# Matrix memory of a two-block model on one core: first head's scores ahead of the gate rows, each head's row spread behind its scores, gate exponential ahead of two value evictions

## The chip, the cores and the metric

One core of a Trainium2 chip runs the whole kernel in one launch. The metric is the device time of an execution in microseconds (us), and the smaller the better. All arithmetic is in 32-bit floats.

## The reference, cut to what matters

The model is a chain of several mixers and feed-forward networks over 256 tokens of width 1024. The change lies in the first mixer alone, a matrix memory (mLSTM) of 4 heads of width 512:

```
xm, z = split(u @ w_in)
xc = silu(causal_conv(xm));  q, k = block_diag(xc);  v = block_diag(xm)
i_pre, f_pre = split(q @ wg_q + k @ wg_k + v @ wg_v + b_gates)
b = cumsum(log_sigmoid(f_pre));  d_log = causal(b[t] - b[s] + i[s])
m_t = max(..., max_s d_log)
scores = (q k^T) * exp(d_log - m_t)
h = (scores v) / max(|sum_s scores|, exp(-m_t))
out = ((layer_norm(h) * norm_w + skip * xc) * silu(z)) @ w_out
```

For each head and each token t, the row values m_t and exp(-m_t) must reach all 128 partitions, since the kernel keeps the keys s on the partitions and the tokens t along the free axis.

## The kernel before, in words

The program is written engine by engine: TensorE (PE), VectorE (DVE), ScalarE (ACT), GpSimd (POOL) and SyncE (SP) each have one list of instructions, executed in the order in which it is written, and semaphores tie them together. There is no planner; the order of the text is the order of the work.

**Banks.** Most PE products go to four PSUM banks in turn. Every product (or group) is a numbered "job" from the list JOBS (line 216); job j uses bank j modulo 4. `wait_free(pe, j)` makes PE wait until job j-4 has been read out, `full` tells that job j is complete, `wait_full(engine, j)` lets the reader wait for that, `out_of` tells that it has been read, and `wait_out` waits for the reading.

**Weights.** SP loads tiles of 1 MB into a ring of six slots (`ring`, line 807), each load released when PE has begun the tile that lets the slot go. Between the pieces of the matrix memory PE executes steps of another product, `ada_step("b", ...)` (matmul at line 1062): the modulation vectors that later layers need. They use two tiles each and a bank of their own, so they wait for nothing of the matrix memory.

**The order on PE around the change** (`stage_mlstm`, from line 1209): query products (1269) with the gate sums (1275), one ada step, the selection of gate rows (1286), eight groups of value products `m_v` (1294), one ada step, the transposed column values `m_cT` (1303), then `m_rows`: for each of the 4 heads one matmul (1309) that spreads two rows of the gates, of 256 tokens each, over the 128 partitions, with 4 rows of contraction and 512 columns. Only then comes the loop over heads: scores (1325, 8 matmuls), one ada step, the sum of the scores (1333), the scores times the values in two groups (1342), the variance of the head before (`head_var`, 1316), one ada step. Every 32-bit matmul stands in the trace as two records, so the 4 row spreads are 8 records.

**DVE** (from 2923) makes the gate rows (2925 to 2947), copies the column values (2950) and the four spread rows out of PSUM (2955), scales the value sums (2984), and adds the causal mask to the first head's row (`decays(0)`, 2962) and centres its values (`centre_values(0)`, 2969). In the head loop it multiplies scores and decay (2992), forms the divisor (2995 to 3000), divides the two groups of outputs (3004), and does `decays(h+1)`, `centre_values(h+1)` and then, from h = 1 on, `head_scale(h-1)` (2974 to 2981: reciprocal and two products over 1024 columns). PE's sum of the scores (1333) waits for 2992.

**ACT** evicts the queries (2293), computes exp and log for the gates (2296, 2299), evicts the eight value groups (2303), then takes the exponential of one gate row (2305), on which 1303 waits, and in the head loop the exponential of the decay (2309), the squares (2339) and the root (2344).

Of the kernel before, what the change touches and what calls it, by code (L numbers as in the profile page):

```python
# [7 lines left out]
P = 128  # L8
F32 = mybir.dt.float32
ALU = mybir.AluOpType  # L10
ACT = mybir.ActivationFunctionType
# [4 lines left out]
T = 256  # L16
# [6 lines left out]
IC = DI // P  # L23
NH = 4
DH = DI // NH
HC = DH // P
# [181 lines left out]
UNDER_INPUT, FIRST_INPUT = 10, 6  # L208
TILES = [("ada_a", 8), ("m_in0", FIRST_INPUT)]
for _s in range(UNDER_INPUT):  # L210
# [3 lines left out]
         ("ada_gap1", 4), ("ffn2", 34), ("ada_gap2", 4), ("hg_z", 8), ("hg_q", 4), ("hg_i", 4), ("hg_g", 4), ("hg_o", 4),  # L214
         ("ffn3", 34)]
JOBS = [("params", 1), ("xT", 4), ("late_params", 4), ("m_in", 2 * INPUT_TILES), ("m_qk", 16), ("m_fsel", 1),
        ("m_v", 8), ("m_cT", 1), ("m_rows", NH), ("m_head", 4 * NH),
        ("m_out", 4), ("ln0", 4), ("ffn0", 4 * FSTEPS - 2), ("s_bT", 8), ("s_cT", 4), ("ln1", 4),
        ("s_direct", 1), ("s_pair", NPAIR), ("glu", 8), ("ln2", 4), ("router", 1), ("u_tok", 4), ("places", 1), ("ctxT", 4), ("ln3", 4), ("rms0", 3),
        ("mla_seq", len(MLA_SEQ) - AH // 2), ("mla_o", 8), ("rms1", 3),  # L220
# [4 lines left out]
def build_program(nc, w, const, out):  # L225

    _, cols = shape_constants()
    tile_of, job_of = reserve(TILES), reserve(JOBS)

    with ExitStack() as ctx:  # L230
        signals = {}

        def S(name):

            if name not in signals:
                signals[name] = ctx.enter_context(nc.semaphore(name))
            return signals[name]
# [93 lines left out]
        def in_job(j):  # L331

            return job_of["m_in"] + 2 * j

        def ffn_job(n):

# [108 lines left out]
        def key_block(a, s):  # L445

            return a[:, s * T:s * T + (P if s else T)]
# [563 lines left out]
        def _(pe):  # L1011
# [197 lines left out]
            def stage_mlstm():  # L1209
# [79 lines left out]
                for g in range(8):  # L1289
# [4 lines left out]
                        last = pe.matmul(bank(j)[:, c * P:(c + 1) * P], xm[:, c0 + c, 4 + a * P:4 + (a + 1) * P],  # L1294
                                         bd[:, 2, c0 + c], start=True, stop=True)
                    full(last, j)
                ada_step("b", UNDER_INPUT + 1, 1)

                j = job_of["m_cT"]
                wait_free(pe, j)  # L1300
                pe.wait_ge(S("gate_rows_ready"), 1)
                for a in range(2):
                    last = pe.matmul(bank(j)[:, a * NH:(a + 1) * NH], gate_rows[0:NH, 4, a * P:(a + 1) * P],
                                     ident[0:NH, 0:NH], start=True, stop=True)
                full(last, j)
                for h in range(NH):
                    j = job_of["m_rows"] + h
                    wait_free(pe, j)
                    full(pe.matmul(bank(j), ident[0:NH, h:h + 1].broadcast_to([NH, P]),
                                   gate_rows[0:NH, 5:7].rearrange("p a t -> p (a t)"), start=True, stop=True), j)  # L1310

                def head_var(h):

# [2 lines left out]
                        last = pe.matmul(psum[:, VAR, 0:T], ones, hsq[:, k], start=k == 0, stop=k == HC - 1)  # L1316
                    last.then_inc(S("h_var_full"), 1)

                wait_out(pe, job_of["m_qk"] + IC - 1)
                for h in range(NH):  # L1320
                    j = job_of["m_head"] + 4 * h
                    wait_free(pe, j)
                    for s in range(2):
                        for c in range(HC):
                            last = pe.matmul(key_block(bank(j), s), xc[:, h * HC + c, s * P:(s + 1) * P],
                                             qk[:, h * HC + c, 0, s * P:T], start=c == 0, stop=c == HC - 1)
                    full(last, j)
                    ada_step("b", UNDER_INPUT + 2 + 2 * h, 1)

                    wait_out(pe, j)  # L1330
                    wait_free(pe, j + 1)
                    for s in range(2):
                        last = pe.matmul(bank(j + 1)[:, s * P:T], ones, key_block(scor[:, h % 2], s), start=s == 0, stop=s == 1,
                                         skip_group_check=True)
                    full(last, j + 1)
                    pe.wait_ge(S("v_centred"), h + 1)
                    for g in range(2):
                        wait_free(pe, j + 2 + g)
                        for e in range(2):
                            for s in range(2):  # L1340
                                at = h * DH + (2 * g + e) * P
                                last = pe.matmul(bank(j + 2 + g)[:, e * T + s * P:(e + 1) * T], vbuf[:, s, at:at + P],
                                                 key_block(scor[:, h % 2], s), start=s == 0, stop=s == 1,
                                                 skip_group_check=True)
                        full(last, j + 2 + g)
                    if h:
                        head_var(h - 1)
                    ada_step("b", UNDER_INPUT + 3 + 2 * h, 1)
# [882 lines left out]
        def _(act):  # L2231
# [36 lines left out]
            def stage_mlstm():  # L2268
# [30 lines left out]
                act.activation(gate_rows[0:NH, 2], gate_rows[0:NH, 2], ACT.Ln, bias=one[0:NH, 0:1]).then_inc(S("ln_f_ready"), 1)  # L2299
                for g in range(8):  # L2300
                    j, s, h = job_of["m_v"] + g, g // 4, g % 4
                    wait_full(act, j)
                    out_of(act.activation(vbuf[:, s, h * DH:(h + 1) * DH], bank(j), ACT.Copy, accum_out=v_sums[:, s, h:h + 1]), j)
                act.wait_ge(S("m_sum_ready"), 1)
                act.activation(gate_rows[0:NH, 6], gate_rows[0:NH, 6], ACT.Exp, scale=-1.0).then_inc(S("gate_rows_ready"), 1)
                for h in range(NH):
                    for s in range(2):
                        act.wait_ge(S("decay_sum_ready"), 2 * h + s + 1)
# [26 lines left out]

            def head_squares(h):

                wait_out(act, job_of["m_head"] + 4 * h + 3)
                act.activation(hsq, hT[:, h * HC:(h + 1) * HC], ACT.Square).then_inc(S("h_sq_ready"), 1)

            def head_root(h):
# [380 lines left out]
        def _(dve):  # L2722
# [136 lines left out]
            def stage_mlstm():  # L2859
# [85 lines left out]
                dve.drain()  # L2945
                dve.tensor_tensor(g[0:NH, 6], g[0:NH, 3], g[0:NH, 5], ALU.add)
                dve.tensor_scalar(g[0:NH, 5], g[0:NH, 5], -1.0, None, ALU.mult).then_inc(S("m_sum_ready"), 1)
                j = job_of["m_cT"]
                wait_full(dve, j)
                out_of(dve.tensor_copy(cT, bank(j)[:, 0:2 * NH].rearrange("p (s h) -> p s h", s=2)), j)  # L2950
                wait_out(dve, job_of["m_qk"] + IC - 1)
                for h in range(NH):
                    j = job_of["m_rows"] + h
                    wait_full(dve, j)
                    out_of(dve.tensor_copy(nm[:, h], bank(j).rearrange("p (k t) -> p k t", k=2)), j)
                dve.wait_ge(S("tables_in"), 16)
                causal = c_("causal").rearrange("p (s t) -> p s t", s=2)

                def decays(h):

                    for s in range(2):
                        dve.tensor_tensor(key_block(decay, s), nm[:, h, 0, s * P:T], causal[:, s, s * P:T], ALU.add
                                          ).then_inc(S("decay_sum_ready"), 1)
# [8 lines left out]
                def head_scale(h):  # L2972
# [7 lines left out]
                    dve.drain()  # L2980
                    dve.tensor_tensor(hh, hh, zs[:, h * HC:(h + 1) * HC], ALU.mult).then_inc(S("h_scaled"), 1)

                wait_out(dve, job_of["m_v"] + 7)
                dve.tensor_scalar(v_sums, v_sums, -1.0 / DH, None, ALU.mult)
                dve.drain()
                decays(0)
                centre_values(0)
                for h in range(NH):
                    j = job_of["m_head"] + 4 * h
                    dve.wait_ge(S("decay_ready"), 2 * h + 2)  # L2990
                    wait_full(dve, j)
                    out_of(dve.scalar_tensor_tensor(scor[:, h % 2], bank(j)[:, 0:CAUSAL], DH ** -0.5, decay, ALU.mult, ALU.mult), j)
                    wait_full(dve, j + 1)

                    dve.tensor_tensor(recip_[:, 0], bank(j + 1)[:, 0:T], nm[:, h, 1], ALU.max)
                    dve.drain()
                    out_of(dve.scalar_tensor_tensor(recip_[:, 0], bank(j + 1)[:, 0:T], -1.0, recip_[:, 0],
                                                    ALU.mult, ALU.max), j + 1)
                    dve.drain()
                    dve.reciprocal(recip_[:, 1], recip_[:, 0])  # L3000
                    dve.drain()
                    for g in range(2):
                        wait_full(dve, j + 2 + g)
                        out_of(dve.tensor_tensor(hT[:, h * HC + 2 * g:h * HC + 2 * g + 2],
                                               bank(j + 2 + g).rearrange("p (a t) -> p a t", a=2),
                                               recip_[:, 1:2].broadcast_to([P, 2, T]), ALU.mult), j + 2 + g)
# [1021 lines left out]
```

## Time and profile before

| | |
|---|---|
| three runs | 2701.3, 2708.13 and 2711.41 us, median 2708.13 |
| span of the profiled execution | 2713.5 us, 5.4 above that median |
| PE busy | 2625.8 us of the span |
| DVE, ACT, POOL busy | 909.8, 404.2, 910.4 us |
| matrix memory from the last query products to the output product | about 184 to 252 us of the span |
| mean granted clock of TensorE | 0.989 of full |

The time of the profiled execution outside its span is not listed. In the profile a line gives the start of a merged group of records, its length, the engine, the line of the code, what it writes and reads, and how often; idle time ahead of it stands in square brackets with what released it. The ends of matmuls are modelled, so lengths are best read as differences between starts.

### The profile page before, as it was taken

What the parts mean: (1) busy time and instruction counts of PE and PEld (TensorE: products, weight loads), DVE (VectorE), ACT (ScalarE), POOL (GpSimd) and SP (SyncE); (2) the same over time, 40 slices, a digit from 0 to 9 for tenths busy, and PEclk for the clock granted to TensorE, in tenths of its full rate; (3) what the DMA queues carried; (4) which work ended last, traced back from release to release, by engine and by line L of the source; (5) the groups of instructions that cost most, each with busy time, mean ns of one, the idle gap of its engine ahead of it and who ended that gap; (6) DMA issues with size and microseconds to landing.
All of it is one profiled execution on the core that took longest, in us unless ns stands there. A gap on an engine that the chain in (4) does not pass through costs nothing.

```text
span 2713.5 us, 47220 instructions
## 1 busy us (share of the span) xinstructions
PE 2625.8 (97%) x20645; PEld 1863.1 (69%) x20645; DVE 909.8 (34%) x1647; ACT 404.2 (15%) x839; POOL 910.4 (34%) x715
## 2 busy tenths in 40 slices
PE   8999999989999999999999999999999999999998
PEld 6767799956644444334445446488888778998998
DVE  4746422384300011100013583222221136522651
ACT  0132010120311000100002344100000121221000
POOL 2662168584000000000000350145555331612886
PEclk9999999999999999999999999999999999999999
DMA  9978545478499999999997210323222243122552
GB/s 299 320 250 287 135 162 164 149 264 280 156 376 407 407 381 385 391 399 406 385 384 249 79 38 16 124 78 93 80 83 86 89 129 109 58 67 93 171 163 87
DMA packets 318303, 561.88 MB, mean 207 GB/s; under 512 B 45544, under 2 KB 181520, under 8 KB 317968
## 3 DMA queue, kind: packets, MB, share of 16 engines
q1 hardware_dynamic: 299280, 554.57, 57.4%
q10 hardware_dynamic: 18816, 4.27, 0.8%
q8 instruction: 164, 2.69, 0.4%
q14 instruction: 43, 0.35, 0.0%
HBM read 557.75 MB, written 1.05 MB: 206 GB/s over the span
## 4 chain that ended last, share of the span: by engine, by line
PE 50%; issue 36%; POOLq 4%; POOL 4%; DVE 2%; DVEq 1%; ACT 1%; DMA 1%; SPq 0%; ACTq 0%
PE psum L1937 10%; PE psum L2166 5%; PE psum L1974 5%; PE psum L2020 4%; PE psum L1021 3%; PE psum L1406 3%; PE psum L2194 2%; PE psum L1359 2%; PE psum L2040 2%; PE psum L1753 2%; POOLq L3767 2%; PE psum L1419 1%; PE psum L2067 1%; PE psum L1244 1%; PE psum L1062 1%
## 5 line engine op out<-in xcount | busy, mean ns | idle before, releaser
L1614 PE MATMUL psum<-ring,xe 128*32 128x512 f32 (+1 forms) x4608 | 458.0, 557 | 2.0 <-issue 1.4
L1614 PEld LDWEIGHTS psum<-ring,xe 128*32 128x32 f32 x4608 | 156.4, 110 | 291.1 <-issue 255.4
L3906 POOL TENSOR_TENSOR ckv<-ckv,nstat 128x512 f32<-128x512 f32 x2 | 2.5, 1265 | 889.9 <-DVE nstat L3413 889.9
L3304 DVE TENSOR_TENSOR act_in<-act_in,psum 128x256 f32<-128x256 f32 (+1 forms) x72 | 28.7, 399 | 629.5 <-ACT act_in L2474 629.5
L1636 PE MATMUL psum<-ring,zs 128*32 128x256 f32 x4224 | 232.3, 379 | 0.2 <-DMA ring<-in_moe_w 0.2
L1636 PEld LDWEIGHTS psum<-ring,zs 128*32 128x32 f32 x4224 | 141.7, 110 | 92.7 <-issue 5.5
L3919 POOL TENSOR_TENSOR w_sums<-ring 128x512 f32<-128x512 f32 (+1 forms) x34 | 42.4, 1247 | 298.1 <-DVE ctxT L3470 124.1
L2474 ACT ACTIVATE act_in<-psum 128x256 f32<-128x256 f32 (+1 forms) x72 | 26.4, 367 | 567.9 <-PE psum L1614 567.9
L1753 PE MATMUL psum<-a,ring 128*128 128x512 f32 x224 | 97.5, 594 | 2.0 <-ACT a L2523 1.3
L3413 DVE RECIPROCAL nstat<-nstat 128x512 f32<-128x512 f32 x23 | 75.8, 3328 | 43.0 <-ACT nstat L2235 43.0
L1937 PE MATMUL psum<-a,w_sums 128*128 128x256 f32 x352 | 83.2, 379 | 2.0 <-ACT a L2523 2.0
L1021 PE MATMUL psum<-a,ring 128*128 128x256 f32 x384 | 84.4, 380 | 0.4 <-DVE a L3669 0.3
L1937 PE MATMUL psum<-a,ring 128*128 128x256 f32 x352 | 80.7, 380 | 2.2 <-DVE a L3384 2.2
L1753 PEld LDWEIGHTS psum<-a,ring 128*128 128x128 f32 x224 | 42.1, 190 | 56.0 <-issue 51.8
L3998 POOL TENSOR_TENSOR w_sums<-ring 128x512 f32<-128x512 f32 (+1 forms) x34 | 42.3, 1244 | 112.1 <-PE psum L2166 51.7
L1021 PEld LDWEIGHTS psum<-a,ring 128*128 128x128 f32 x384 | 72.4, 190 | 10.8 <-DVE a L3669 1.2
L1937 PE MATMUL psum<-x_rows,w_sums 128*128 128x256 f32 x352 | 79.6, 379 | 0.0
L1419 PE MATMUL psum<-zs,ring 128*128 128x256 f32 x352 | 77.8, 379 | 0.0
L1937 PEld LDWEIGHTS psum<-a,ring 128*128 128x128 f32 x352 | 66.5, 190 | 12.3 <-DVE a L3384 2.8
L1937 PEld LDWEIGHTS psum<-a,w_sums 128*128 128x128 f32 x352 | 66.8, 190 | 11.4 <-issue 2.4
L1937 PEld LDWEIGHTS psum<-x_rows,w_sums 128*128 128x128 f32 x352 | 66.9, 190 | 9.1
L1419 PEld LDWEIGHTS psum<-zs,ring 128*128 128x128 f32 x352 | 66.0, 190 | 8.5
(612 smaller groups left out, 4892.6 us busy)
## 6 DMA issues: line engine op xcount, KB each, us to landing
ring<-in_moe_w SPq DMA_DIRECT2D x216, 1024.0 KB, 11.2
ring<-in_ffn_w SPq DMA_DIRECT2D x97, 1024.0 KB, 5.2
ring<-in_ada_w SPq DMA_DIRECT2D x96, 1024.0 KB, 8.4
ring<-in_moe_w SPq DMA_DIRECT2D x64, 768.0 KB, 6.6
ring<-in_hg_w_in SPq DMA_DIRECT2D x20, 1024.0 KB, 5.1
ring<-in_mlstm_w_in SPq DMA_DIRECT2D x16, 1024.0 KB, 9.2
ring<-in_mlstm_w_out SPq DMA_DIRECT2D x8, 1024.0 KB, 7.7
ring<-in_s_w_glu SPq DMA_DIRECT2D x8, 1024.0 KB, 11.7
```

Of the source, the lines that this page charges most:

```text
L1021: last = pe.matmul(bank(j)[:, n * T:(n + 1) * T], tile[:, k * width + n * P:k * width + (n + 1) * P], src(k), start=start and k == 0, stop ...
L1359: last = pe.matmul(bank(j)[:, n * T:(n + 1) * T], ring[:, t % RING, k * 256 + n * P:k * 256 + (n + 1) * P], hT[:, 8 * half + k], start=hal ...
L1406: last = pe.matmul(ffn_product(n, m), held[:, k], moving(k), start=k == 0, stop=k == 3)
L1419: last = pe.matmul(psum[:, NB + n // 2, (n % 2) * T:(n % 2 + 1) * T], ring[:, t % RING, k * D + n * P:k * D + (n + 1) * P], hid[:, i % 2, ...
L1614: last = pe.matmul(psum[rows, r, 0:2 * nb * 32].rearrange("p (u b f) -> p u b f", u=2, b=nb), xe[:, k, at:at + 32], tile[:, :, :, rows], s ...
L1636: last = pe.matmul(psum[32 * b:32 * b + 32, DOWN + r // 2, (r % 2) * T:(r % 2 + 1) * T], turned[:, r, at:at + 32], ring[:, t % RING, a:a + T],
L1753: last = pe.matmul(bank(j), ring[:, t % RING, at:at + P], src(k), start=k == 0, stop=k == kc - 1)
L1937: last = pe.matmul(product_bank(side, m), held[:, k], moving(k), start=k == 0, stop=k == 3)
L1974: last = pe.matmul(product_bank(q, m), held[:, k, q], moving(2 * kk + k), start=kk == 0 and k == 0 and m in (1, 5, 3, 6), stop=kk == 5, sk ...
L2020: last = pe.matmul(product_bank(side, m), held[:, k], moving(k), start=k == 0, stop=k == 3)
L2166: last = pe.matmul(small_bank(side, m), held[:, k], moving(k), start=k == 0, stop=k == 3)
L3413: dve.reciprocal(st, st).then_inc(S("nrstd_ready"), 1)
```

## The change

It renumbers the jobs: `m_cT`, `m_rows` and the 16 head jobs, 21 in all, become one list of 21 in the new order of use. On PE the first head's scores come directly behind the value products; then the column values; then the row spread of head 0; then the ada step that stood in front of the column values. In the head loop, each further head's row spread stands directly behind its scores. On DVE, the copy of a head's spread rows moves into `decays(h)`, with a drain behind it; `decays(0)` moves ahead of the wait for the last value eviction. The places of the calls `decays(h+1)`, `centre_values(h+1)` and `head_scale(h-1)` in the DVE loop stay. On ACT, the gate exponential moves from behind the eighth value eviction to between the sixth and the seventh. Every matmul, copy and activation of before is still there; the only new instructions are the four drains on DVE, one behind each copy.

```
-        ("m_v", 8), ("m_cT", 1), ("m_rows", NH), ("m_head", 4 * NH),
+        ("m_v", 8), ("m_head", 5 * NH + 1),

+        def head_job(kind, h):
+            return job_of["m_head"] + {"scores": 5 * h + 1 if h else 0, "cT": 1, "rows": 5 * h + 2, "sums": 5 * h + 3,
+                                       "values": 5 * h + 4}[kind]

 PE, behind the value products:
-                ada_step("b", UNDER_INPUT + 1, 1)
-                j = job_of["m_cT"]
+                def head_scores(h):
+                    j = head_job("scores", h)
+                    wait_free(pe, j)
+                    for s in range(2):
+                        for c in range(HC):
+                            last = pe.matmul(key_block(bank(j), s), xc[:, h * HC + c, s * P:(s + 1) * P],
+                                             qk[:, h * HC + c, 0, s * P:T], start=c == 0, stop=c == HC - 1)
+                    full(last, j)
+                def head_rows(h):
+                    j = head_job("rows", h)
+                    wait_free(pe, j)
+                    full(pe.matmul(bank(j), ident[0:NH, h:h + 1].broadcast_to([NH, P]),
+                                   gate_rows[0:NH, 5:7].rearrange("p a t -> p (a t)"), start=True, stop=True), j)
+                wait_out(pe, job_of["m_qk"] + IC - 1)
+                head_scores(0)
+                j = head_job("cT", 0)
                 wait_free(pe, j)
                 pe.wait_ge(S("gate_rows_ready"), 1)
...
-                for h in range(NH):
-                    j = job_of["m_rows"] + h
-                    wait_free(pe, j)
-                    full(pe.matmul(bank(j), ident[0:NH, h:h + 1].broadcast_to([NH, P]), ...), j)
+                head_rows(0)
+                ada_step("b", UNDER_INPUT + 1, 1)
...
                 for h in range(NH):
...
-                    ada_step("b", UNDER_INPUT + 2 + 2 * h, 1)
-                    wait_out(pe, j)
+                    if h:
+                        head_scores(h)
+                        head_rows(h)
+                    ada_step("b", UNDER_INPUT + 2 + 2 * h, 1)
+                    j = head_job("sums", h)
+                    wait_out(pe, head_job("scores", h))

 ACT:
                 for g in range(8):
                     j, s, h = job_of["m_v"] + g, g // 4, g % 4
+                    if g == 6:
+                        act.wait_ge(S("m_sum_ready"), 1)
+                        act.activation(gate_rows[0:NH, 6], gate_rows[0:NH, 6], ACT.Exp, scale=-1.0).then_inc(S("gate_rows_ready"), 1)
                     wait_full(act, j)
                     out_of(act.activation(vbuf[:, s, h * DH:(h + 1) * DH], bank(j), ACT.Copy, accum_out=v_sums[:, s, h:h + 1]), j)
-                act.wait_ge(S("m_sum_ready"), 1)
-                act.activation(gate_rows[0:NH, 6], ..., ACT.Exp, scale=-1.0).then_inc(S("gate_rows_ready"), 1)

 DVE:
-                for h in range(NH):
-                    j = job_of["m_rows"] + h
+                dve.wait_ge(S("tables_in"), 16)
+                causal = c_("causal").rearrange("p (s t) -> p s t", s=2)
+                def decays(h):
+                    j = head_job("rows", h)
                     wait_full(dve, j)
                     out_of(dve.tensor_copy(nm[:, h], bank(j).rearrange("p (k t) -> p k t", k=2)), j)
-                dve.wait_ge(S("tables_in"), 16)
-                causal = c_("causal").rearrange("p (s t) -> p s t", s=2)
-                def decays(h):
+                    dve.drain()
                     for s in range(2):
                         dve.tensor_tensor(key_block(decay, s), nm[:, h, 0, s * P:T], causal[:, s, s * P:T], ALU.add
...
+                decays(0)
                 wait_out(dve, job_of["m_v"] + 7)
                 dve.tensor_scalar(v_sums, v_sums, -1.0 / DH, None, ALU.mult)
                 dve.drain()
-                decays(0)
                 centre_values(0)
```

## Rows read from the trace of the kernel before

**Rows 1.** The page: busy us of each engine, share of the span, instructions.

```profile
PE 2625.8 (97%) x20645; PEld 1863.1 (69%) x20645; DVE 909.8 (34%) x1647; ACT 404.2 (15%) x839; POOL 910.4 (34%) x715
```

**Rows 2.** PE in order of time, 195 to 232 us: start, length, group, count.

```profile
195.24 1.92 PE L1062 MATMUL psum<-ring,csil_one 128*32 128x512 f32 x16
197.90 0.57 PE L1303 MATMUL psum<-cst,act_in 4*128 4x4 f32 x4 [0.74 <-ACT act_in L2305]
198.34 4.83 PE L1309 MATMUL psum<-act_in,cst 4*128 4x512 f32 x8
203.10 5.06 PE L1325 MATMUL psum<-qk,xc 128*128 128x256 f32 x16
...
209.94 0.92 PE L1333 MATMUL psum<-bd,cst 128*128 128x256 f32 x4
...
215.26 2.88 PE L1325 MATMUL psum<-qk,xc 128*128 128x256 f32 x16
218.08 1.92 PE L1062 MATMUL psum<-ring,csil_one 128*32 128x512 f32 x16
219.94 0.92 PE L1333 MATMUL psum<-bd,cst 128*128 128x256 f32 x4
...
225.13 1.92 PE L1062 MATMUL psum<-ring,csil_one 128*32 128x512 f32 x16
...
229.80 1.92 PE L1062 MATMUL psum<-ring,csil_one 128*32 128x512 f32 x16
231.66 0.92 PE L1333 MATMUL psum<-bd,cst 128*128 128x256 f32 x4
```

**Rows 3.** PE's weight loads in order of time, during the row spreads.

```profile
199.29 0.18 PEld L1309 LDWEIGHTS psum<-act_in,cst 4*128 4x128 f32 x1 [0.24 <-issue]
199.72 0.18 PEld L1309 LDWEIGHTS psum<-act_in,cst 4*128 4x128 f32 x1 [0.24 <-issue]
```

**Rows 4.** Stretches: from:to, us, busy of PE, PEld, DVE, ACT, POOL; granted clock, DMA share, GB/s.

```profile
159.10:163.60 4.50, 4.50 (x25) 4.50 (x26) 1.57 (x8) 1.59 (x4) 0.01 (x1) 0.62 0.89 329
195.30:197.20 1.90, 1.86 (x17) 0.35 (x16) 0.00 (x0) 1.84 (x3) 1.90 (x3) 1.00 0.00 0
201.00:203.10 2.10, 2.10 (x4) 0.34 (x2) 0.72 (x2) 0.00 (x0) 2.10 (x3) 0.50 1.05 396
203.10:208.10 5.00, 5.00 (x19) 4.16 (x19) 2.46 (x6) 0.80 (x2) 5.00 (x6) 0.55 0.05 18
```

**Rows 5.** ACT in order of time, 194 to 198 us.

```profile
194.45 0.60 ACT L2303 ACTIVATE vbuf<-psum 128x512 f32<-128x512 f32 x1 [0.18 <-PE psum L1294]
...
196.05 1.28 ACT L2305 ACT_TABLE_LOAD   x1
197.34 0.41 ACT L2305 ACTIVATE act_in<-act_in 4x256 f32<-4x256 f32 x1
```

**Rows 6.** DVE in order of time, 194 to 231 us.

```profile
194.09 0.39 DVE L2947 TENSOR_SCALAR act_in<-act_in 4x256 f32<-4x256 f32 x1
...
203.21 0.69 DVE L2955 COPY bd<-psum 128x512 f32<-128x512 f32 x1 [1.01 <-PE psum L1309]
...
204.59 1.15 DVE L2969 TENSOR_SCALAR vbuf<-vbuf,small 128x512 f32<-128x512 f32 x2
...
224.94 0.62 DVE L2962 TENSOR_TENSOR bd<-bd,cst 128x256 f32<-128x256 f32 x2
...
226.26 1.75 DVE L2976 RECIPROCAL bd<-bd 128x256 f32<-128x256 f32 x1
228.08 1.23 DVE L2978 TENSOR_TENSOR qk<-qk,bd 128x1024 f32<-128x1024 f32 x1
...
230.53 0.55 DVE L2992 SCALAR_TENSOR_TENSOR bd<-psum,bd 128x384 f32<-128x384 f32 x1
```

**Rows 7.** PE in order of time, 159 to 172 us: input products behind a wait for POOL.

```profile
159.08 4.57 PE L1244 MATMUL psum<-qk 128*128 128x128 f32 x24 [2.66 <-POOL qk L3780]
...
169.11 2.84 PE L1244 MATMUL psum<-qk 128*128 128x128 f32 x24
```

More of the change, by code:

```diff
@@ L1305, in stage_mlstm @@
                 full(last, j)
-                for h in range(NH):
-                    j = job_of["m_rows"] + h
-                    wait_free(pe, j)
-                    full(pe.matmul(bank(j), ident[0:NH, h:h + 1].broadcast_to([NH, P]),
-                                   gate_rows[0:NH, 5:7].rearrange("p a t -> p (a t)"), start=True, stop=True), j)
+                head_rows(0)
+                ada_step("b", UNDER_INPUT + 1, 1)
                 def head_var(h):
@@ L1317, in head_var @@
                     last.then_inc(S("h_var_full"), 1)
-                wait_out(pe, job_of["m_qk"] + IC - 1)
                 for h in range(NH):
-                    j = job_of["m_head"] + 4 * h
+                    if h:
[4 more added lines that the diff above has]
+                    wait_out(pe, head_job("scores", h))
                     wait_free(pe, j)
                     for s in range(2):
-                        for c in range(HC):
-                            last = pe.matmul(key_block(bank(j), s), xc[:, h * HC + c, s * P:(s + 1) * P],
-                                             qk[:, h * HC + c, 0, s * P:T], start=c == 0, stop=c == HC - 1)
+                        last = pe.matmul(bank(j)[:, s * P:T], ones, key_block(scor[:, h % 2], s), start=s == 0, stop=s == 1,
+                                         skip_group_check=True)
                     full(last, j)
-                    ada_step("b", UNDER_INPUT + 2 + 2 * h, 1)
-                    wait_out(pe, j)
[L1331 to L1335, printed above, removed]
                     pe.wait_ge(S("v_centred"), h + 1)
+                    j = head_job("values", h)
                     for g in range(2):
-                        wait_free(pe, j + 2 + g)
+                        wait_free(pe, j + g)
                         for e in range(2):
@@ L1341, in stage_mlstm @@
                                 at = h * DH + (2 * g + e) * P
-                                last = pe.matmul(bank(j + 2 + g)[:, e * T + s * P:(e + 1) * T], vbuf[:, s, at:at + P],
+                                last = pe.matmul(bank(j + g)[:, e * T + s * P:(e + 1) * T], vbuf[:, s, at:at + P],
                                                  key_block(scor[:, h % 2], s), start=s == 0, stop=s == 1,
                                                  skip_group_check=True)
-                        full(last, j + 2 + g)
+                        full(last, j + g)
                     if h:
@@ L2301, in stage_mlstm @@
                     j, s, h = job_of["m_v"] + g, g // 4, g % 4
+                    if g == 6:
+                        act.wait_ge(S("m_sum_ready"), 1)
+                        act.activation(gate_rows[0:NH, 6], gate_rows[0:NH, 6], ACT.Exp, scale=-1.0).then_inc(S("gate_rows_ready"), 1)
                     wait_full(act, j)
                     out_of(act.activation(vbuf[:, s, h * DH:(h + 1) * DH], bank(j), ACT.Copy, accum_out=v_sums[:, s, h:h + 1]), j)
-                act.wait_ge(S("m_sum_ready"), 1)
-                act.activation(gate_rows[0:NH, 6], gate_rows[0:NH, 6], ACT.Exp, scale=-1.0).then_inc(S("gate_rows_ready"), 1)
                 for h in range(NH):
@@ L2336, in head_squares @@
             def head_squares(h):
-                wait_out(act, job_of["m_head"] + 4 * h + 3)
+                wait_out(act, head_job("values", h) + 1)
                 act.activation(hsq, hT[:, h * HC:(h + 1) * HC], ACT.Square).then_inc(S("h_sq_ready"), 1)
@@ L2947, in stage_mlstm @@
                 dve.tensor_scalar(g[0:NH, 5], g[0:NH, 5], -1.0, None, ALU.mult).then_inc(S("m_sum_ready"), 1)
-                j = job_of["m_cT"]
+                j = head_job("cT", 0)
                 wait_full(dve, j)
@@ L2951, in stage_mlstm @@
                 wait_out(dve, job_of["m_qk"] + IC - 1)
-                for h in range(NH):
-                    j = job_of["m_rows"] + h
-                    wait_full(dve, j)
-                    out_of(dve.tensor_copy(nm[:, h], bank(j).rearrange("p (k t) -> p k t", k=2)), j)
                 dve.wait_ge(S("tables_in"), 16)
@@ L2959, in decays @@
                 def decays(h):
+                    j = head_job("rows", h)
+                    wait_full(dve, j)
+                    out_of(dve.tensor_copy(nm[:, h], bank(j).rearrange("p (k t) -> p k t", k=2)), j)
+                    dve.drain()
                     for s in range(2):
@@ L2985, in stage_mlstm @@
                 dve.drain()
-                decays(0)
                 centre_values(0)
                 for h in range(NH):
-                    j = job_of["m_head"] + 4 * h
+                    j = head_job("scores", h)
                     dve.wait_ge(S("decay_ready"), 2 * h + 2)
@@ L2992, in stage_mlstm @@
                     out_of(dve.scalar_tensor_tensor(scor[:, h % 2], bank(j)[:, 0:CAUSAL], DH ** -0.5, decay, ALU.mult, ALU.mult), j)
-                    wait_full(dve, j + 1)
-                    dve.tensor_tensor(recip_[:, 0], bank(j + 1)[:, 0:T], nm[:, h, 1], ALU.max)
+                    j = head_job("sums", h)
+                    wait_full(dve, j)
+                    dve.tensor_tensor(recip_[:, 0], bank(j)[:, 0:T], nm[:, h, 1], ALU.max)
                     dve.drain()
-                    out_of(dve.scalar_tensor_tensor(recip_[:, 0], bank(j + 1)[:, 0:T], -1.0, recip_[:, 0],
-                                                    ALU.mult, ALU.max), j + 1)
+                    out_of(dve.scalar_tensor_tensor(recip_[:, 0], bank(j)[:, 0:T], -1.0, recip_[:, 0],
+                                                    ALU.mult, ALU.max), j)
                     dve.drain()
@@ L3001, in stage_mlstm @@
                     dve.drain()
+                    j = head_job("values", h)
                     for g in range(2):
-                        wait_full(dve, j + 2 + g)
+                        wait_full(dve, j + g)
                         out_of(dve.tensor_tensor(hT[:, h * HC + 2 * g:h * HC + 2 * g + 2],
-                                               bank(j + 2 + g).rearrange("p (a t) -> p a t", a=2),
-                                               recip_[:, 1:2].broadcast_to([P, 2, T]), ALU.mult), j + 2 + g)
+                                               bank(j + g).rearrange("p (a t) -> p a t", a=2),
+                                               recip_[:, 1:2].broadcast_to([P, 2, T]), ALU.mult), j + g)
                     if h + 1 < NH:
```

## The prediction

> **What bounds the kernel now.** I read the page first. PE is busy for 2625.8 of 2713.5 us [rows 1], so what counts is what keeps PE waiting or slow. Then PE's list in order of time around the change [rows 2], PE's weight loads there [rows 3], the granted clock by stretches [rows 4], and ACT's and DVE's lists [rows 5, 6], each to see which of them is late where PE waits. The span lies 5.4 us above the median of the runs; all sums below are differences against the profiled execution, put on the median of 2708.13. A measurement of this kernel can tell about 0.5% from no change, 13.5 us.
>
> Three things are to be seen. First, ahead of the heads PE waits 0.74 us for the gate exponential, since ACT loads its table (1.28 us) and computes it (0.41 us) only behind the last value eviction, though DVE had delivered its input at 194.09 + 0.39 [rows 2, 5, 6]. Second, the column values and the four spreads use 4 of 128 rows, and behind them the clock falls: 0.50 (1.2 of 2.4 GHz) from 201.0 to 203.1, 0.55 until 208.1 [rows 4]. The scores of head 0 start at 203.10 and their successor sums only at 209.94; the scores of head 1 take 218.08 - 215.26 = 2.82 us, those of head 0 take 5.06 by their length [rows 2]. Third, in the loop PE runs gapless: from the sums of head 1 (219.94) to those of head 2 (231.66) are 11.72 us [rows 2], and DVE finishes what the sums wait for at 230.53 + 0.55 = 231.08 [rows 6]. **DVE is only 0.6 us ahead of PE there**, and it is free to be so because its next mask addition starts at 224.94 [rows 6] on a row that was spread long before.
>
> **Part 1, the first head.** Before, PE needs 209.94 - 195.24 = 14.70 us from the ada step to the sums. At full clock the same work is: ada step with the wait, 197.90 - 195.24 = 2.66; column values 198.34 - 197.90 = 0.44; four spreads; scores 2.82; one ada step, 231.66 - 229.80 = 1.86 [rows 2]. A record of a spread takes 199.72 - 199.29 = 0.43 us, a spread of two records 0.86, four 3.44 [rows 3]. Sum 11.22, so the slow clock cost 3.48.
> After, from 195.24: scores 2.82, column values 0.44, one spread 0.86, two ada steps 3.72, sum 7.84, and the sums start at 203.08, **6.86 us earlier**. Of it 2.58 are three spreads that come back later, about 0.8 the wait, 3.5 the clock.
> The covers: ACT's table load starts when its sixth eviction is out, about 194.3 (the row at 194.45 is the seventh); 1.28 + 0.41 give 196.0 [rows 5], and PE wants it at 195.24 + 2.82 = 198.06. Two value evictions move behind it and end near 197.3; their reader, DVE's scaling of value sums, comes after 200. That edit costs nothing while 2 us of scores cover it; uncovered it would cost at most its 1.69. DVE gets the spread at 199.36; before, from the start of its last copy to the start of centring are 204.59 - 203.21 = 1.38 us, then centring 1.15 and the product 0.55 (the loop's) [rows 6]; with 0.1 for signals the sums could start at 202.6. PE's 203.08 is later, by 0.5.
> The ada steps' weights: DMA stands still at 195.3 to 197.2 [rows 4], so the ring is full when they are wanted later than before. I cost the move of the ada step past SP's queue at nothing. Were the ring short by a tile, a megabyte at the 396 GB/s of rows 4 is 2.6 us; the longer loop below makes that less likely.
>
> **Part 2, head 1.** The spread adds 0.86 to PE. DVE stands in `decays(1)` until it is complete, then needs: signal 0.05, copy 0.69, drain 0.07 (228.08 - 226.26 - 1.75), then what is 230.53 + 0.55 - 224.94 = 6.14 in the loop, less the head scaling that head 1 has not (230.53 - 226.26 = 4.27), so 1.87, and 0.1 back to PE: 2.78 [rows 6]. PE covers one ada step, 1.86. Wait 0.92. **Later by 1.8.**
>
> **Part 3, heads 2 and 3.** The added wait is `wait_full` on the spread inside `decays(h+1)`. Queued behind it on DVE stand the copy, the mask, `centre_values`, the whole `head_scale` of the head before, and the product that the next sums wait for. None of these but the first two needs the spread. PE delivers the spread only behind variance, ada step and scores: for head 2 at (229.80 - 219.94) + 0.86 = 10.72 us after the sums of head 1 [rows 2], while DVE used to go on at 224.94, 5.0 after them. From there 0.05 + 0.69 + 0.07 + 6.14 + 0.1 = 7.05 us, of which PE covers 1.86: it waits 5.2 us. With the spread, 6.05 for each head, twice: **later by 12.1.** ACT's exponential lies beside centring and scaling, as before. POOL's additions and the output product follow DVE as before; nothing behind head 3 takes it back, since the loads follow PE's progress and the ring is full.
>
> **Part 4, the clock of the two waits.** What falls behind a wait of 5.2 us is not in the loop of before. From below, nothing: the 0.74 us wait ahead of 197.90 was itself followed by full clock [rows 2, 4]. From above, by a row: behind a wait of 2.66 us for POOL the same 24 records took 4.57 instead of 2.84, 1.73 us more, at a granted 0.62 [rows 4, 7]; behind the dip at 201 the scores took 5.06 instead of 2.88, 2.2 more [rows 2]. Both rows are nearer to a 5.2 us wait than the short one, so I take their middle, 1.95, twice: 3.9. The Trainium skill speaks against this change here (TensorE: Matmul & The Clock Gate, section on HAM oscillation): a loop whose matmul bursts are parted by long waits falls to 1.2 GHz and pays the ramp again in every turn. By it both waits pay in full; the trace agrees so far as its 2.66 us wait did.
>
> **Sum.** -6.86 + 1.8 + 12.1 + 3.9 = +10.9. Predicted 2708.1 + 10.9 = 2719, which is 0.4% slower, within what counts as the same. Without a clock price it is +7.0 (2715), with 2.2 twice +11.4.
>
> **The rivals.**
> *The slow clock lasts through the burst.* Behind each wait the sums, values and variance are 225.13 - 219.94 = 5.2 us at full clock [rows 2]. If all of it runs at 1.2 GHz, each wait costs 5.2 more instead of 1.95: +7.0 + 10.4 = +17.4, 2725.5. This ends on the slower side. Its place is the stretch from the sums of heads 2 and 3 to the next ada step, and it decides once the dips cost over 3.2 us each. For it: the first dip lasted from about 201 to 208 [rows 4]. Against: dense work ended it, and each stall here is followed by dense work.
> *The wait of DVE is covered.* If the copy came early enough, only part 1 and three spreads would remain, -6.86 + 2.58 = -4.3, 2704. Against it: PE's text puts the spread behind the scores and DVE's text puts everything behind the spread, and no engine reorders its list in these rows.
> *The first head gains no clock.* Column values, a spread and two ada steps follow the first scores; if the clock falls there as before, 3.5 come back: +14.4, 2722.5. For it: 1.3 us of 4-row work. Against: that was 3.9 us before, behind a wait, and scores now stand ahead of it.
>
> **How the numbers follow.** The forecast 0.67, the lasting slow clock 0.18, no gain of clock at the first head 0.08, the covered wait 0.07. The forecast's own range is its clock from 0 to 2.2 with the runs' own spread of some 5 us: 2710 to 2725. The range takes in the rival above: 2709 to 2727. Slower by over 0.5%: all of the lasting clock, half of the third rival, and 0.05 of the forecast by its edge, 0.27. Faster by over 0.5% is left only if something unseen is added to the covered wait, 0.03. The same: 0.70.
>
> **What would show it.** In the new profile: the sums of head 0 start near 203; a full granted clock from 199 to 207; DVE's copy of each spread row waits for PE, the second to fourth for 4 to 6 us; PE waits about 0.9 us at the sums of head 1 and about 5 at those of heads 2 and 3, released by DVE's product of scores and decay; the sums stand some 17.8 us apart for heads 1 to 2 and 2 to 3 in place of 11.72; a dip of granted clock behind each of these two. It would be wrong if the head loop were still gapless, if the sums of head 0 came at 206 or later, or if DMA released any of these waits.

## The result, and the profile after

The changed kernel takes 2717.5 us (median of 6 runs, 2714.81 to 2724.47) against 2706.2 us of the kernel before (6 runs, 2701.3 to 2711.41): ratio 1.0047, interval 1.0034 to 1.006. That is slower by 11.3 us by the medians and by some 13 by the ratio. The forecast was 2719, 10.9 above the median that the first three runs of before had (2708.13), in the range 2709 to 2727.

Both profiled executions reach this part at slightly different times (the changed one 4.98 us earlier). Of that, 1.6 us are the dip of the clock in the input products [rows 7], which its execution didn't have; the rest comes from elsewhere ahead of this part and is not followed up. So everything below is told from landmarks inside the part: from the end of the value products, where PE turns to the ada step (before) or to the first scores (after), to the start of the output product. That was 252.16 - 195.24 = 56.92 us before, and is 260.60 - 190.26 = 70.34 now, **13.4 longer**.

PE in order of time in the changed kernel; columns are start, length, group, count, and in brackets the idle time ahead with what released it (L1309 scores, L1326 column values, L1317 spread, L1067 ada step, L1349 sums, L1359 values, L1336 variance, L1376 output product):

```profile
190.26 2.78 PE L1309 MATMUL psum<-qk,xc 128*128 128x256 f32 x16
192.97 0.60 PE L1326 MATMUL psum<-cst,act_in 4*128 4x4 f32 x4
193.44 1.10 PE L1317 MATMUL psum<-act_in,cst 4*128 4x512 f32 x2
194.47 3.64 PE L1067 MATMUL psum<-ring,csil_one 128*32 128x512 f32 x32
198.21 0.92 PE L1349 MATMUL psum<-bd,cst 128*128 128x256 f32 x4
...
210.58 0.92 PE L1349 MATMUL psum<-bd,cst 128*128 128x256 f32 x4 [1.26 <-DVE bd L3011]
...
220.45 1.12 PE L1317 MATMUL psum<-act_in,cst 4*128 4x512 f32 x2
221.50 1.92 PE L1067 MATMUL psum<-ring,csil_one 128*32 128x512 f32 x16
228.60 1.65 PE L1349 MATMUL psum<-bd,cst 128*128 128x256 f32 x4 [5.17 <-DVE bd L3011]
230.04 4.75 PE L1359 MATMUL psum<-bd,vbuf 128*128 128x256 f32 x16
234.62 1.89 PE L1336 MATMUL psum<-bd,cst 128*128 128x256 f32 x8
...
249.26 1.65 PE L1349 MATMUL psum<-bd,cst 128*128 128x256 f32 x4 [5.17 <-DVE bd L3011]
...
260.60 14.06 PE L1376 MATMUL psum<-qk,ring 128*128 128x256 f32 x64
```

Against [rows 2]: the first four lines are gapless and at full clock, where the kernel before waited and then ran slow. But the loop, gapless before, now has a wait of 1.26 us and two of 5.17 us, all for L3011, DVE's product of scores and decay. And behind the long waits PE is slow: the 16 values take 4.75 in place of 2.78.

Stretches of the same profile (from:to, us, busy of PE, PEld, DVE, ACT, POOL, then granted clock, DMA share, GB/s): the first head, the first long wait with what follows it, and what follows the second.

```profile
190.26:198.21 7.95, 7.85 (x56) 4.07 (x54) 3.47 (x8) 2.78 (x8) 7.63 (x8) 1.00 0.17 41
...
223.40:228.60 5.20, 0.03 (x5) 0.00 (x1) 4.99 (x6) 2.49 (x3) 0.44 (x1) 0.87 1.04 384
228.60:236.45 7.85, 7.85 (x29) 6.59 (x29) 3.98 (x5) 0.00 (x0) 1.91 (x1) 0.65 0.18 64
249.26:257.02 7.76, 7.76 (x28) 6.50 (x29) 3.98 (x5) 0.00 (x0) 1.90 (x1) 0.66 0.23 74
```

PE is idle while DVE is busy all through the wait; the clock falls within it (0.87 as the mean of the wait), and sums, values and variance take 7.85 and 7.76 us at a granted 0.65 and 0.66, where the same work took 5.19 before (219.94 to 225.13 in [rows 2]).

What DVE does around the first long wait, in order of time (L2977 copy of the spread, L2981 mask, L2988 centring, L2995 to L3000 head scaling, L3011 product):

```profile
221.61 0.69 DVE L2977 COPY bd<-psum 128x512 f32<-128x512 f32 x1 [5.94 <-PE psum L1317]
222.40 0.63 DVE L2981 TENSOR_TENSOR bd<-bd,cst 128x256 f32<-128x256 f32 x2
222.94 0.88 DVE L2988 TENSOR_SCALAR vbuf<-vbuf,small 128x512 f32<-128x512 f32 x2
223.73 1.75 DVE L2995 RECIPROCAL bd<-bd 128x256 f32<-128x256 f32 x1
225.55 1.23 DVE L2997 TENSOR_TENSOR qk<-qk,bd 128x1024 f32<-128x1024 f32 x1
226.85 1.23 DVE L3000 TENSOR_TENSOR qk<-qk,zs 128x1024 f32<-128x1024 f32 x1
227.99 0.55 DVE L3011 SCALAR_TENSOR_TENSOR bd<-psum,bd 128x384 f32<-128x384 f32 x1
```

The two engines wait for each other by turns: DVE stands 5.94 us for a spread that PE places behind its scores, then PE stands 5.17 us for work that DVE had queued behind that spread. In [rows 6] DVE went from the values of a head into the mask without a wait.

### The profile page after: what moved, and what is told of

Its sections match the earlier page's. It is cut to its first block, busy times and chain, and to the rows that moved or that the text cites. A ratio compares the mean times of both kernels' runs of the same rounds, so it can differ in the third digit from the quotient of the medians.

```text
span 2719.6 us, 47223 instructions
## 1 busy us (share of the span) xinstructions
PE 2622.0 (96%) x20645; PEld 1859.2 (68%) x20645; DVE 905.6 (33%) x1647; ACT 403.7 (15%) x839; POOL 911.3 (34%) x715
## 3 DMA queue, kind: packets, MB, share of 16 engines
HBM read 557.75 MB, written 1.05 MB: 205 GB/s over the span
## 4 chain that ended last, share of the span: by engine, by line
PE 48%; issue 36%; POOLq 5%; POOL 4%; DVE 4%; DVEq 1%; ACT 1%; DMA 1%; SPq 0%; ACTq 0%
PE psum L1954 10%; PE psum L2183 5%; PE psum L1991 5%; PE psum L2037 3%; PE psum L1026 3%; PE psum L1423 3%; PE psum L2211 2%; PE psum L1376 2%; PE psum L2057 2%; PE psum L1770 2%; POOLq L3788 2%; PE psum L1436 1%; PE psum L2084 1%; POOLq L3928 1%; PE psum L1890 1%
```

## The experiments

Each is told by its ratio to the kernel before and by the same local time, from the end of the value products to the output product.

**1. Head scaling ahead of the wait for the spread.** DVE's order alone is changed:

```
-                    if h + 1 < NH:
-                        decays(h + 1)
-                        centre_values(h + 1)
                     if h:
                         head_scale(h - 1)
+                    if h + 1 < NH:
+                        decays(h + 1)
+                        centre_values(h + 1)
```

> The changed kernel with one thing altered on DVE: in the head loop head_scale(h-1) stands ahead of decays(h+1) and centre_values(h+1). Theory (DVE's in-order wait for the spread holds up work that doesn't need it): head scaling is then done while the spread is still to come, and only copy, mask, centring and product stay behind it. PE's waits at the sums of heads 2 and 3 fall from 5.17 us to about 1.3, as at head 1; sums of head 1 to sums of head 2 take about 14.2 us in place of 18.02; the clock doesn't fall there. From the sums of head 0 to the output product some 13 us shorter than in the changed kernel; the whole about 0.5 us over the kernel before, ratio to it 1.000. Rival (the reading of the spread itself, or the extra drain, is what is slow): the waits stay over 4 us and the ratio stays 1.0047.

Measured: ratio 1.0011 (1.0002 to 1.002); local time 243.84 - 185.90 = 57.94 us, 12.4 less than the changed kernel and 1.0 more than before. PE around head 2:

```profile
206.22 0.92 PE L1349 MATMUL psum<-bd,cst 128*128 128x256 f32 x4 [1.26 <-DVE bd L3011]
...
220.65 0.92 PE L1349 MATMUL psum<-bd,cst 128*128 128x256 f32 x4 [1.59 <-DVE bd L3011]
221.41 2.78 PE L1359 MATMUL psum<-bd,vbuf 128*128 128x256 f32 x16
```

From sums to sums are 14.43 us in place of 18.02, and the values behind a wait of 1.59 take their full-clock 2.78. The spread is as late as ever; only the 4.3 us of scaling no longer stand behind it. From the sums of head 0 to the output product the changed kernel takes 20.2 us more than before (62.39 against 42.22), and this order of work on DVE takes 12.4 of them away, as the theory had it. What is left of them is the three spreads, 3.2 us, and three short waits, 4.4. The ratio is 0.001 over the one named. The wait is 0.3 longer than expected: POOL now runs at the same time as the mask, which takes 0.7 us more by it, while the centring, slowed at head 1, is not slowed here (see the last section).

**2. The spread ahead of variance, ada step and scores.** DVE stays as changed, the job numbers of spread and scores change places, and on PE:

```
                         full(last, j + g)
+                    if h + 1 < NH:
+                        head_rows(h + 1)
                     if h:
                         head_var(h - 1)
...
                     if h:
                         head_scores(h)
-                        head_rows(h)
```

> The changed kernel with the spread of head h+1 put right behind the values of head h, ahead of variance, ada step and scores; the job numbers follow. Theory (the spread comes too late, not too dear): DVE finds it ready when it gets there, no wait of PE in the head loop, 11.72 + 1.05 = 12.8 us from the sums of head 1 to those of head 2, no fall of the clock. Against the kernel before: -6.75 us at the first head and three spreads of 1.05 us back, -3.6 us, ratio 0.9987; against the changed kernel -17 us. Rival (splitting the spreads over the loop costs by itself, by small matmuls between large ones or by the clock): no faster than the kernel before, ratio 1.001 or more.

> The kernel with the spread behind the values once more, since its interval touched 1.0. If its local gain of 3.2 us is real in the whole time, the ratio is again 0.998 to 0.9995; if that was chance, it is 1.000 or more.

Measured: 0.9991 (0.9982 to 1.0) the first time, 0.9988 (0.9979 to 0.9997) the second. Local times 238.96 - 185.25 = 53.71 and 243.31 - 189.59 = 53.72 us, 3.2 less than before, where 3.6 were expected. PE, first run:

```profile
204.25 0.92 PE L1348 MATMUL psum<-bd,cst 128*128 128x256 f32 x4
205.01 2.78 PE L1358 MATMUL psum<-bd,vbuf 128*128 128x256 f32 x16
207.72 1.12 PE L1317 MATMUL psum<-act_in,cst 4*128 4x512 f32 x2
...
217.22 0.92 PE L1348 MATMUL psum<-bd,cst 128*128 128x256 f32 x4
```

and DVE in the same time, which copies the spread (L2978) without a wait:

```profile
208.05 1.29 DVE L3026 TENSOR_TENSOR qk<-psum,bd 128x512 f32<-128x512 f32 x2
209.26 0.68 DVE L2978 COPY bd<-psum 128x512 f32<-128x512 f32 x1
```

No wait is left: 217.22 - 204.25 = 12.97 from sums to sums. The change's gain at the first head is real and is kept here; its loss was the place of three small matmuls. This version is 0.6% faster than the changed kernel. Against the kernel before it is about 0.1% faster: one interval touches 1.0, the other stays just under it.

**3. The spread ahead of the scores only.** A position between the two, which asks whether the wait follows from the spread's time as a sum. On PE `head_rows(h)` and `head_scores(h)` change places, and their job numbers with them.

```
                     if h:
-                        head_scores(h)
                         head_rows(h)
+                        head_scores(h)
```

> The changed kernel with the spread of heads 1 to 3 ahead of their scores instead of behind them, otherwise as the change has it: 2.8 us earlier than in the change, 4.7 us later than in the run with the spread behind the values. Theory (the wait is the spread's lateness carried through DVE's chain): for heads 2 and 3 the spread is complete 8.2 us after the sums of the head before, DVE's chain of 7.05 us puts the product at 15.3, PE could start at 12.8, so it waits about 2.4 us there and not at all at head 1; sums of head 1 to sums of head 2 take 15.3 us in place of 18.02. A wait of 2.66 us was followed by a fall of the clock in the input products before, so a fall is likely but not sure here; with it at both heads up to 4 us. Against the kernel before, from the end of the value products to the output product: +2 us without, +6 with the falls, ratio 1.001 to 1.0025. Rival (the position among large matmuls matters in itself): the waits stay at 5.17 us, or are gone.

Measured: ratio 1.0009 (1.0 to 1.0017); local time 248.30 - 188.46 = 59.84 us, 2.9 more than before. The waits are 2.36 us at both heads, as summed, and there is none at head 1.

```profile
222.65 0.92 PE L1349 MATMUL psum<-bd,cst 128*128 128x256 f32 x4 [2.36 <-DVE bd L3011]
...
237.86 0.92 PE L1349 MATMUL psum<-bd,cst 128*128 128x256 f32 x4 [2.36 <-DVE bd L3011]
```

The clock behind two equal waits, in stretches from the sums to the next ada step:

```profile
222.65:227.85 5.20, 5.20 (x28) 4.46 (x28) 3.89 (x5) 0.00 (x0) 1.92 (x1) 1.00 1.04 381
237.86:244.72 6.86, 6.86 (x28) 5.76 (x28) 3.99 (x5) 0.00 (x0) 1.91 (x1) 0.75 0.72 228
```

It fell behind one and not behind the other, within one execution: at 2.36 us the clock can go either way, and the one fall cost 6.86 - 5.20 = 1.66 us. What decides between the two is not shown.

**4. The waits filled.** 22 unused products of the identity by itself ahead of the sums of heads 2 and 3 keep PE busy while DVE is late:

```
+                    if h >= 2:
+                        spare_products(psum[:, NB, 0:P], 22)
                     j = head_job("sums", h)
                     wait_out(pe, head_job("scores", h))
```

> The changed kernel with 22 products of identity by identity (128x128, results unused, about 4.7 us) ahead of the sums of heads 2 and 3, so that PE is busy during most of DVE's lateness. Theory (the waits cost twice, once by themselves and once by the clock): the sums start at the same distance as before this edit, 18 us after those of head 1, but the granted clock stays full, and sums, values and variance take 5.2 us in place of 7.85 at both heads: 5.3 us less than the changed kernel, ratio to the kernel before 1.0027. Rival (the clock's fall has nothing to do with the waits): the granted clock still falls at both and the time is that of the changed kernel, 1.0047.

Measured: ratio 1.0033 (1.0021 to 1.0045); local time 251.17 - 186.05 = 65.12 us, 5.2 less than the changed kernel.

```profile
206.37 0.92 PE L1351 MATMUL psum<-bd,cst 128*128 128x256 f32 x4 [1.25 <-DVE bd L3013]
...
219.14 5.18 PE L1113 MATMUL psum<-cst 128*128 128x128 f32 x44
224.38 0.92 PE L1351 MATMUL psum<-bd,cst 128*128 128x256 f32 x4
```

```profile
224.38:229.58 5.20, 5.20 (x29) 4.46 (x29) 3.89 (x5) 0.00 (x0) 1.91 (x1) 1.00 0.25 92
```

The sums come as late as without the filling, 18.01 us after those of head 1, and what follows them takes 5.20 in place of 7.85 (at head 3 too, 5.20 in place of 7.76). So idle PE is what lets the clock fall here, and of the change's local loss the clock is 5.2 us.

**5. The exponential alone.** In the kernel before, the two lines of the gate exponential are moved between the sixth and seventh eviction, nothing else:

```
                 for g in range(8):
                     j, s, h = job_of["m_v"] + g, g // 4, g % 4
+                    if g == 6:
+                        act.wait_ge(S("m_sum_ready"), 1)
+                        act.activation(gate_rows[0:NH, 6], ..., ACT.Exp, scale=-1.0)
...
-                act.wait_ge(S("m_sum_ready"), 1)
-                act.activation(gate_rows[0:NH, 6], ..., ACT.Exp, scale=-1.0)
```

> The kernel before with the gate exponential alone moved between the sixth and seventh value eviction; the column values stay behind the ada step, the four spreads behind them. Theory (PE waits there for the table load alone, and the clock falls because of the 4-row products): the 0.74 us wait is gone, from the ada step to the sums of head 0 takes 13.9 us in place of 14.70, and the clock still falls to 1.2 GHz behind the spreads. Rival (the wait is what lets the clock fall): the fall goes too, and it takes 10.4 us.

Measured: ratio 0.9994 (0.9984 to 1.0004), not clear of 1; local time 245.51 - 191.05 = 54.46 us, 2.5 less than before. The numbering is that of the kernel before: L1303 column values, L1309 spreads, L1325 scores, L1333 sums.

```profile
191.05 1.92 PE L1062 MATMUL psum<-ring,csil_one 128*32 128x512 f32 x16
192.90 0.60 PE L1303 MATMUL psum<-cst,act_in 4*128 4x4 f32 x4
193.37 3.67 PE L1309 MATMUL psum<-act_in,cst 4*128 4x512 f32 x8
196.97 4.53 PE L1325 MATMUL psum<-qk,xc 128*128 128x256 f32 x16
...
203.29 0.92 PE L1333 MATMUL psum<-bd,cst 128*128 128x256 f32 x4
```

```profile
195.50:196.97 1.47, 1.47 (x4) 0.37 (x2) 1.25 (x2) 0.00 (x0) 1.30 (x2) 0.98 1.05 407
196.97:200.00 3.03, 3.03 (x8) 2.49 (x8) 2.46 (x6) 0.80 (x2) 3.03 (x4) 0.50 0.76 286
```

The wait of 0.74 is gone, and the clock still falls, the theory's way; but only as the four spreads end (granted 0.98 until 196.97, 0.50 behind it; before it was down from 201.0 on, with 2 us of spreads to come), and for a shorter time. The stretch takes 203.29 - 191.05 = 12.24 us, about midway between the 13.9 of the theory and the 10.4 of the rival. The clock cost 1.7 here and not 3.5. So the wait isn't needed for the fall; whether it made the fall of before the longer one, or the 3.5 varies by itself, one execution doesn't tell.

**6. The loop's part alone.** The first head in the order of before (ada step, column values, one spread, scores; exponential behind the last eviction), the other spreads behind their scores; the job numbers of the first head follow:

```
-                wait_out(pe, job_of["m_qk"] + IC - 1)
-                head_scores(0)
+                ada_step("b", UNDER_INPUT + 1, 1)
                 j = head_job("cT", 0)
...
                 head_rows(0)
-                ada_step("b", UNDER_INPUT + 1, 1)
+                wait_out(pe, job_of["m_qk"] + IC - 1)
+                head_scores(0)
```

> The loop's part of the change alone: first head in the order of before (ada step, column values, one spread, scores), exponential behind the last eviction, but spreads of heads 1 to 3 behind their scores. Theory: from the sums of head 0 to the output product as in the changed kernel, 62.4 us against 42.2 before. Ahead of it, with one spread in place of four, the clock has less cause to fall: 14.70 - 2.6 = 12.1 us to the sums with the fall, 8.6 without. Which of the two comes tells whether the four spreads in a row are needed for the fall. Rival for the loop: the waits of 5.17 us came from the shifted start of the first head, and are under 2 us here.

Measured: ratio 1.0055 (1.0039 to 1.0072); from the sums of head 0 to the output product 258.21 - 195.96 = 62.25 us, as in the changed kernel (62.39), with the same two waits of 5.17, and 7.99 and 7.82 us of sums, values and variance behind them. The rival, a shifted start, is out. Ahead of the sums:

```profile
189.83 0.57 PE L1325 MATMUL psum<-cst,act_in 4*128 4x4 f32 x4 [0.74 <-ACT act_in L2322]
190.26 1.10 PE L1317 MATMUL psum<-act_in,cst 4*128 4x512 f32 x2
191.29 2.88 PE L1309 MATMUL psum<-qk,xc 128*128 128x256 f32 x16
...
195.96 0.92 PE L1349 MATMUL psum<-bd,cst 128*128 128x256 f32 x4
```

The wait of 0.74 is back, one spread follows it, and the scores take 2.8 us at full clock: 195.96 - 187.16 = 8.80 us from the ada step to the sums, against the 8.6 named for no fall. With run 5 this says what the fall of [rows 4] went with: the four spreads in a row (3.60 us in run 5), with or without the short wait, and not one spread with it. That the scores now stand ahead of the spread, as the prediction argued, isn't what keeps the clock up: here they stand behind it. Each of these is one execution. It also says that the first head's new order is worth little beyond this: 8.80 against 7.95 in the changed kernel, and 0.74 of that is the wait for the exponential.

Not tried: all four spreads behind the first scores, as one block. With four banks taken in turn, the third spread would, by the job numbers, wait for the bank of the first scores until DVE has read them; it would need other banks. So what the block would cost there is open.

## Why the prediction was right

It was right in its mechanism and nearly in its size. That the forecast of 2719 lies only 1.5 us above the measured 2717.5 is partly luck: its base of three runs was 1.9 us above the median of six, and its sum was below what the same stretch shows. Term by term:

| term | foretold | measured |
|---|---|---|
| first head, to its sums | -6.86 | 7.95 - 14.70 = -6.75 |
| head 1, sums to sums | +1.8, wait 0.92 | 12.37 - 10.00 = +2.37, wait 1.26 |
| head 2, sums to sums | +6.05, wait 5.2 | 18.02 - 11.72 = +6.30, wait 5.17 |
| head 3, without the clock | +6.05, wait 5.2 | 20.66 - 11.72 - 2.66 = +6.28, wait 5.17 |
| clock, both | +3.9 | 2.66 + 2.57 = +5.2 |
| in all | +10.9 | +13.4 locally; by the ratio 9.2 to 16.2 |

(The first clock fall lies between the sums of heads 2 and 3, which stand 20.66 us apart; the prediction's sign of 17.8 for both distances had left its own dip out. The second, 2.57, lies behind the sums of head 3: 260.60 - 249.26 = 11.34 against 8.78.)

**Part 1** held in its size, with the clock at 1.00 over the whole first head. But the sums were to be bound by PE, with 0.5 us to spare on DVE, and that reserve wasn't there: DVE's product ends at 198.16, just ahead of the sums at 198.21, and PE is busy for 7.85 of the 7.95 us.

```profile
197.62 0.54 DVE L3011 SCALAR_TENSOR_TENSOR bd<-psum,bd 128x384 f32<-128x384 f32 x1
```

From the start of its copy (194.68) DVE took 3.48 us to there, and 3.08 were summed. The cover of the exponential held with room: it ends at 191.1 in the new trace, and PE wants it at 192.97. That DMA costs nothing held too: no wait of PE in this part is released by a load.

**Parts 2 and 3**, the wait inside `decays(h+1)` with the scaling queued behind it, is what runs 1, 2 and 3 show from three sides: take the scaling from behind it, or the spread from behind the scores, and the waits go to 1.6 and to none; at the position between they are 2.36 where the same sum gave 2.4. Two terms were too small by a few tenths. A spread occupies 221.50 - 220.45 = 1.05 us and not 0.86, since the pitch of 0.43 in [rows 3] doesn't hold the change from one shape of work to the next. And at head 1 the centring takes 1.23 us, not 0.88; in run 6, where it takes 0.88, the wait at head 1 is 0.91, the 0.92 of the sum.

**Part 4** is the term that was mis-sized. I took 1.95 for each fall, the middle of two rows behind shorter waits or other work; it was 2.66 and 2.57. The upper bound of 2.2 was no bound: it counted only the scores, 2.9 us of work, in a dip that part 1 itself prices at 3.48 as a whole, while 5.2 us of work stand behind each wait here. The rule of the Trainium skill that stood against this change (TensorE: Matmul & The Clock Gate, section on HAM oscillation) came true: the trace agrees, two waits of 5.17 us, two falls, and two more in run 6. Run 4 shows that these were the waits' doing. The rival of a slow clock through the whole burst (5.2 each) came half true: each fall cost about half of that, and the variance behind the values runs at its full-clock 1.83 us (234.62 to 236.45).

The rival of the first head's clock didn't happen: one spread and the column values are not enough for a fall, in this kernel as in run 6.

## What to carry to other kernels

When a small producer moves closer to its consumer, look at what its reader has queued behind the wait: an in-order engine turns the lateness of one small result into lateness of everything written after it, needed or not. Place the producer by the time at which the reader comes to it (here behind the values, 5 us after the sums), not by what it is grouped with in the text, and put independent work in front of a wait rather than behind it. A wait of TensorE can cost twice: here each of the two waits of 5.17 us cost half as much again through the clock, and of two waits of 2.36 us one did and one didn't.

## What was not expected of the hardware

Some of DVE's work is slower while POOL works. The centring of two tiles of 128x512 took 1.15 us from start to start at head 1 with POOL busy for 0.95 of it, and 0.79 at head 2 with POOL idle (from:to, us, busy of PE, PEld, DVE, ACT, POOL, changed kernel):

```profile
208.84:209.99 1.15, 0.49 (x8) 0.00 (x0) 1.15 (x3) 1.15 (x3) 0.95 (x1) 1.00 1.06 390
222.94:223.73 0.79, 0.49 (x8) 0.00 (x0) 0.79 (x3) 0.79 (x3) 0.00 (x0) 1.00 1.04 384
```

Run 6 has the same centring of head 1 at the same place in DVE's list, but POOL is done by then. It takes 0.79, and PE waits 0.91 us behind it in place of 1.26:

```profile
206.59:207.38 0.79, 0.49 (x8) 0.00 (x0) 0.79 (x4) 0.79 (x3) 0.00 (x0) 1.00 1.02 376
```

```profile
207.98 0.92 PE L1349 MATMUL psum<-bd,cst 128*128 128x256 f32 x4 [0.91 <-DVE bd L3010]
```

In run 1 the mask was slow: DVE's two additions of 128x256 took 1.31 us where they overlapped POOL's addition of head outputs, against 0.63 in the changed kernel (POOL's list first, then DVE's).

```profile
216.48 2.38 POOL L3822 TENSOR_TENSOR qk<-qk 128x1024 f32<-128x1024 f32 x1 [11.05 <-DVE qk L3000]
```

```profile
218.03 1.31 DVE L2981 TENSOR_TENSOR bd<-bd,cst 128x256 f32<-128x256 f32 x2
```

It looks as if the mask waits until POOL's instruction on 128x1024 is over: in run 1 the next work of DVE starts at 219.26, 0.40 us behind POOL's end. In run 2 the mask of head 1 took 2.34 us beside such an instruction of POOL, and DVE again went on 0.40 us behind POOL's end (201.25 against 200.85). Not all of DVE's work is slowed: with POOL busy throughout, the reciprocal took the same 1.75 us as with POOL idle (from 200.19 and from 212.56 in the changed kernel). No run takes POOL's work away by itself, so that POOL is the cause rests on these overlaps and on run 6.

The clock can fall although PE is never idle: in run 5 PE is busy without a gap from 191.05 on, the clock is full while the first of the 4-row products run, and it is down when the fourth spread ends. And equal waits of 2.36 us in one execution (run 3) were followed once by a fall and once by none.
